# One-hot tiles built for four quads at a time, key sums by halving, and routing keys turned one group earlier

## The reference, cut to what matters

```python
q = (xb @ w_q).reshape(128, 8, 2, 128)
s = einsum('bhpd,hpkd->bhpk', q, sub_keys)      # two score lists of 128 keys per head
sv, si = top_k(s, 16)
cand = sv[:, :, 0, :, None] + sv[:, :, 1, None, :]
cv, ci = top_k(cand, 16)
i1 = take_along_axis(si[:, :, 0], ci // 16)
i2 = take_along_axis(si[:, :, 1], ci % 16)
idx = i1 * 128 + i2                             # 8 heads x 16 experts per token
gate = softmax(cv)
act = gelu(einsum('bhkd,bd->bhk', u_emb[idx], xb))
out = einsum('bhk,bhkd->bd', gate * act, v_emb[idx])
```

## Time and profile before

| what | us |
|---|---|
| median of 3 runs | 2011.41 |
| lowest and highest of them | 2003.05, 2014.95 |
| the profiled execution | 2016.21 |
| its span, first to last instruction | 2014.5 |
| PE, DVE, ACT, POOL busy | 1926.0, 1462.6, 751.0, 738.8 |
| mean granted TensorE clock | 0.981 of full speed |

### The profile page before, as it was taken

One profiled execution on the slowest core, in us unless ns is written; L12 is line 12 of the kernel. 1 busy time (PEld: TensorE's weight loads), 2 busy tenths in 40 slices (PEclk: granted clock), 3 DMA queues, 4 the chain that ended last, 5 costly groups with the idle time before them and its releaser, 6 DMA issues.

```text
span 2014.5 us, 35532 instructions
## 1 busy us (share of the span) xinstructions
PE 1926.0 (96%) x14267; PEld 1758.4 (87%) x14267; DVE 1462.6 (73%) x2696; ACT 751.0 (37%) x953; POOL 738.8 (37%) x600
## 2 busy tenths in 40 slices
PE   9998987888999999999999999998899999999997
PEld 8998976767459999988888888888899999999997
DVE  6616664775247778878887997885698788888887
ACT  6334543443032133445444545543223332233323
POOL 8235737560023101322322241221488544333440
PEclk9999988999999999999999999999999999999999
DMA  6212210020231135677888797779999999999993
GB/s 204 64 45 76 66 40 2 9 92 12 71 142 59 68 132 193 237 275 276 330 326 295 274 366 268 287 282 341 356 367 362 386 364 362 360 365 368 358 336 124
DMA packets 179180, 450.11 MB, mean 223 GB/s; under 512 B 15729, under 2 KB 92273, under 8 KB 168817
## 3 DMA queue, kind: packets, MB, share of 16 engines
q1 hardware_dynamic: 125472, 240.77, 34.5%
q0 software_dynamic: 42496, 151.03, 20.3%
q10 hardware_dynamic: 11088, 56.63, 6.9%
HBM read 383.26 MB, written 65.07 MB: 223 GB/s over the span
## 4 chain that ended last, share of the span: by engine, by line
PE 77%; DVE 9%; POOL 4%; DMA 3%; ACT 3%; issue 3%; SPq 1%; ACTq 0%; DVEq 0%; POOLq 0%
PE bank L2028 27%; PE bank L1943 23%; PE bank L1897 5%; PE bank L1360 5%; PE bank L1849 3%; DMA v_raw<-in_pv 2%; PE bank L1952 2%; PE bank L1380 1%; DMA sca<-in_pu_rows,pick 1%; PE bank L1919 1%; DVE u_lo L2602 1%; DVE sca L2608 1%; DVE pre L2166 1%; SPq L595 1%; PE bank L1570 1%
## 5 line engine op out<-in xcount | busy, mean ns | idle before, releaser
L1943 PE MATMUL bank<-xhi,u_hi 128*128 128x448 f32 x1008 | 380.0, 377 | 5.2 <-ACT actb L1236 5.2
L1943 PE MATMUL bank<-xhi,u_lo 128*128 128x448 f32 x1008 | 369.8, 367 | 0.0
L1943 PE MATMUL bank<-xlo,u_hi 128*128 128x448 f32 x1008 | 368.7, 366 | 0.0
L842 POOL DMA_INDIRECT sca<-in_pu_rows,pick x128 | 173.1, 1352 | 527.9 <-DVE sdot L2608 414.1
L2028 PE MATMUL bank<-w_hi,v_hi 128*128 128x416 f32 x1024 | 358.3, 350 | 6.1 <-DVE w_lo L2861 5.4
L2028 PE MATMUL bank<-w_lo,v_hi 128*128 128x416 f32 x1024 | 357.8, 349 | 0.0
L2028 PE MATMUL bank<-w_hi,v_lo 128*128 128x416 f32 x1024 | 357.7, 349 | 0.0
L1289 ACT ACTIVATE v_hi<-v_raw 128x4096 fp32r<-128x4096 f32 x32 | 115.9, 3621 | 394.1 <-PE bank L2028 355.7
L2867 DVE TENSOR_TENSOR v_lo<-v_raw,v_hi 128x4096 fp32r<-128x4096 f32 x32 | 141.6, 4425 | 95.7 <-ACT v_hi L1289 95.7
L2602 DVE TENSOR_TENSOR u_lo<-u_raw,u_hi 128x2048 fp32r<-128x2048 f32 x64 | 146.5, 2290 | 86.8 <-ACT u_hi L1208 82.5
L1943 PEld LDWEIGHTS bank<-xhi,u_hi 128*128 128x128 f32 x1008 | 189.7, 188 | 19.6 <-issue 5.6
(11 more groups left out here) (698 smaller groups left out, 3728.7 us busy)
## 6 DMA issues: line engine op xcount, KB each, us to landing
u_raw<-in_pu SPq DMA_DIRECT2D x64, 1024.0 KB, 5.1
v_raw<-in_pv SPq DMA_DIRECT2D x128, 512.0 KB, 8.6
act_scratch<-actb ACTq DMA_DIRECT2D x64, 448.0 KB, 6.1
wts<-act_scratch SPq DMA_DIRECT2D x32, 896.0 KB, 6.9
gate_scratch<-gst ACTq DMA_DIRECT2D x13, 2048.0 KB, 9.0
gring<-gate_scratch SPq DMA_DIRECT2D x32, 832.0 KB, 13.4
wring<-in_w_q SPq DMA_DIRECT2D x4, 2048.0 KB, 8.9
wp_raw<-in_w_in SPq DMA_DIRECT2D x7, 1024.0 KB, 5.4
```

The lines of the kernel that those rows point to most:

```text
L842: pool.indirect_dma_start(rows_u[s % RING], None, pu_rows[:, :], bass.IndirectOffsetOnAxis(pick[:, s:s + 1], 0)).then_inc(s_row[s % RING], 16)
L1943: ins = mm(bank[b][:, 0:DS], lhsT, rhs[:, 0:DS], **on)
```

## The change

1. One block of one-hots is made for four quads: `hot_b` and `hot_e` have 2048 elements in one operation, `hot_a` is made for two quads at a time, and "hots_ready" goes up by two. The rings grow with it: `hot_b` holds 8 quads (from 4), `hot_a` 4 (from 2), `hot_e` 4 (from 2).
2. `hot_b` and `hot_a` move to SBUF addresses that held query data used up by then; `hot_e` takes their old place.
3. `sum_keys` is one reduce no more, but four additions of 2048, 1024, 512 and 256 elements, each waiting for the one before.
4. PE turns the keys of position 1 ahead of group 11, and those of position p+1 ahead of the last group of position p. PE's code for positions 1 and 2 is written out, where it was a loop over 8 groups.

```diff
-        hot_b = sb("hot_b", [128, 8, 128, 2], f16, scope=first)
-        hot_a = sb("hot_a", [128, 2, 2, 2, 128, 2], f16, scope=first)
-        hot_e = sb("hot_e", [128, 4, 128, 2], f16, scope=first)
+        hot_e = sb("hot_e", [128, 8, 128, 2], f16, scope=first)
+        sb("gap_hot", [128, 1536], scope=first)
...
+        hots = ExitStack()
+        hot_b = sb("hot_b", [128, 16, 128, 2], f16, scope=hots)
+        hot_a = sb("hot_a", [128, 4, 2, 2, 128, 2], f16, scope=hots)
...
+            def turn_keys(pos):
+                t = ORDER[pos]
+                n = FTILES[t][1]
+                pe.wait_ge(S("routed"), ROUTED[pos])
+                for a, src in enumerate((isel[0:n, 0, :], isel[0:n, 1, :], gate[0:n, t, :])):
+                    ins = pe.transpose(bank[4][:, 128 * a:128 * a + n], src, ident[0:n, 0:n])
+                ins.then_inc(S("hk_done"), 1)
...
+            for e in range(GU):
+                dots(0, 2, HEAD0 - 2, e)
+            turn_keys(1)
+            for e in range(GU):
+                dots(0, 2, HEAD0 - 1, e)
+            for pos in range(1, 5):
+                for g in range(G0[pos], G0[pos] + GROUPS_OF[pos]):
+                    if pos < 4 and g + 1 == G0[pos + 1]:
+                        turn_keys(pos + 1)
+                    first_q, last_q = QUAD0[g - HEAD0], QUAD0[g - HEAD0 + 1]
+                    half = (last_q - first_q) // 2
+                    for e in range(GU):
+                        dots(0, 2, g, e)
+                        for quad in range(first_q + half * e, first_q + half * e + half):
+                            gate_quad(quad)
...
-                    if k % 2 == 0:
...
-                        if quad >= 4:
-                            dve.wait_ge(S("gmat_done"), quad - 2)
-                        TT(hot_b[:, s:s + 4, :, :], every, both[1], ALU.is_equal)
+                    if k % 4 == 0:
...
+                        if quad >= 8:
+                            dve.wait_ge(S("gmat_done"), quad - 4)
+                        TT(hot_b[:, s:s + 8, :, :], every, both[1], ALU.is_equal)
...
-                    if quad >= 2:
-                        dve.wait_ge(S("gmat_done"), quad - 1)
...
+                    if k % 2 == 0:
+                        if quad >= 4:
+                            dve.wait_ge(S("gmat_done"), quad - 2)
+                        rows_e = hot_e[:, 2 * (k % 4):2 * (k % 4) + 4, :, :]
+                        two = hot_a[:, quad % 4:quad % 4 + 2, :, :, :, :].rearrange("p q r a n j -> p (q r) a n j")
+                        TT(two, rows_e.unsqueeze(2).to_broadcast([128, 4, 2, 128, 2]),
+                           hk_g[:, 2 * k:2 * k + 4, :, :].unsqueeze(3).to_broadcast([128, 4, 2, 128, 2]), ALU.mult
+                           ).then_inc(S("hots_ready"), 2)
...
-                link(dve.tensor_reduce(isel[0:n, :, :].rearrange("p a (k r) -> p (a k) r", r=2),
-                                       hot[0:n, :].rearrange("p (k j r) -> p k r j", k=128, j=16), AX.X, ALU.add))
+                places = hot[0:n, :].rearrange("p (k j r) -> p k j r", k=128, j=16)
+                for half in (8, 4, 2):
+                    link(TT(places[:, :, 0:half, :], places[:, :, 0:half, :], places[:, :, half:2 * half, :], ALU.add))
+                link(TT(isel[0:n, :, :].rearrange("p a (k r) -> p (a k) r", r=2), places[:, :, 0, :], places[:, :, 1, :], ALU.add))
```

More of the change, by code:

```diff
@@ L39 @@
 TAIL = 3
+ROUTED = [1, 2, 3, 4, 5]
 G0 = [HEAD0 + sum(GROUPS_OF[:t]) for t in range(5)]
@@ L344, in hybrid_step @@
         query.close()
+        hots = ExitStack()
+        hot_b = sb("hot_b", [128, 16, 128, 2], f16, scope=hots)
+        hot_a = sb("hot_a", [128, 4, 2, 2, 128, 2], f16, scope=hots)
+        hots.close()
         first.close()
@@ L1944, in dots, with gate_quad @@
                 ins.then_inc(S("dots_done"), 1)
-            def gate_quad(i, t, k):
-                pe.wait_ge(S("hots_ready"), i * 16 + (32 * t + k + 1))
-                pe.wait_ge(S("gmat_copied"), i * 16 + (32 * t + k + 1))
+            def gate_quad(k):
+                pe.wait_ge(S("hots_ready"), k + 1)
+                pe.wait_ge(S("gmat_copied"), k + 1)
                 for j in range(4):
                     for part in range(2):
-                        ins = mm(bank[5 + k % 2][:, 128 * j:128 * j + 128], hot_b[:, 2 * (k % 4) + j // 2, :, j % 2],
-                                 hot_a[:, k % 2, j // 2, part, :, j % 2], start=part == 0, stop=part == 1)
+                        ins = mm(bank[5 + k % 2][:, 128 * j:128 * j + 128], hot_b[:, 2 * (k % 8) + j // 2, :, j % 2],
+                                 hot_a[:, k % 4, j // 2, part, :, j % 2], start=part == 0, stop=part == 1)
                 ins.then_inc(S("gmat_done"), 1)
@@ L1972, in _ @@
                 dots(0, 2, 1, e)
-            with pe.Fori(0, HEAD0 // 2 - 1) as i:
+            def turn_keys(pos):
[5 more added lines that the diff above has]
+                ins.then_inc(S("hk_done"), 1)
+            with pe.Fori(0, HEAD0 // 2 - 2) as i:
                 for q in range(2):
@@ L1976, in _ @@
                         dots(i, 2, 2 + q, e)
[L1977 to L2000, removed]
+            for e in range(GU):
[13 more added lines that the diff above has]
+                            gate_quad(quad)
             for g in range(GATED_END, UG):
                 for e in range(GU):
-                    dots(0, 8, g, e)
+                    dots(0, 2, g, e)
             pe.sem_inc(S("sum_done"), 2 * KD)
@@ L2664, in one_hots @@
                     quad = t0 // 4 + k
-                    s = 2 * (quad % 4)
-                    if k % 2 == 0:
-                        both = [hk_ab[:, a, 4 * k:4 * k + 8].rearrange("p (r j) -> p r j", j=2).unsqueeze(2)
-                                .to_broadcast([128, 4, 128, 2]) for a in range(2)]
-                        every = lanes[:, :, :].unsqueeze(1).to_broadcast([128, 4, 128, 2])
-                        if quad >= 4:
-                            dve.wait_ge(S("gmat_done"), quad - 2)
-                        TT(hot_b[:, s:s + 4, :, :], every, both[1], ALU.is_equal)
+                    s = 2 * (quad % 8)
+                    if k % 4 == 0:
+                        both = [hk_ab[:, a, 4 * k:4 * k + 16].rearrange("p (r j) -> p r j", j=2).unsqueeze(2)
+                                .to_broadcast([128, 8, 128, 2]) for a in range(2)]
+                        every = lanes[:, :, :].unsqueeze(1).to_broadcast([128, 8, 128, 2])
+                        if quad >= 8:
+                            dve.wait_ge(S("gmat_done"), quad - 4)
+                        TT(hot_b[:, s:s + 8, :, :], every, both[1], ALU.is_equal)
                         if quad:
```

## The result

The changed kernel takes **2030.76 us** in the median of 4 runs (2029.24 to 2036.34), the kernel before 2012.7 (2003.05 to 2014.95). The ratio is 1.009, with a 95% interval of 1.0062 to 1.0117: slower, and by more than the 0.5% that the prediction took as what can be told from no change. The forecast was 2015.8, with 2026 as the upper end. The same comparison made once more later, beside other runs of the kernel before, gave 1.0053 (1.0032 to 1.0074): slower too, but there the 0.5% lies inside the interval.

A forecast was written before the change was run, and what follows sets the result against it. PE was taken to bound the kernel. The terms, 2 x (0.97 + 1.59) + 0.97 - 1.64 = +4.4 us, gave 2020.6 for the profiled execution and a median of 2015.8; range 2004 to 2025.4, 2026 with the unrolling's bad end.

The forecast's parts named there:

- What bounds the kernel: PE, busy 1926.0 of 2014.5 us; DVE's saved 11 us count nothing, covered by 59.5 us of waits for `u_hi`.
- Price of a doubled operation: On DVE, 2048 elements take 1.22 us, 1.14 to a successor, 1.26 to a waiting one; 11 us of DVE time saved.
- the additions: On DVE in j = 11: four additions hold it 2.9 us where the reduce held it 4.44.
- Price of the longer block: On DVE, 3.67 us until the first quad can start, for 2.08: 1.59 us later.
- j = 10: Group in positions 1, 2 and 3: the long block makes the first quad's stall 1.80 us, from 0.21.
- j = 11 and the head of position 4: No stall at j = 11 in positions 1 to 3; position 4's first quad just in time, -1.64 us.
- j = 14: Group in positions 1 and 2: the stall of 1.57 us becomes 3.16, +1.59 each.
- In positions 2 and 3 the first block gets longer too, behind four dots; I find some 0.5 us left, and count 0: First quads of positions 2 and 3: some 0.5 us of room for the longer block, so 0 us.
- rival C: Gathers collide with long blocks (first quads of positions 2, 3; j = 14): 9.6 us more, 2025.4; chance 0.13.
- Addresses: 0; the new places are idle: Moving the one-hot buffers to other SBUF addresses costs 0 us.
- Written-out code, 0: PE's written-out code in positions 1 and 2 costs 0; bad end 0.1 us per group, +3.

The follow-up runs named there:

- e10: Kernel before with 1.46 us of useless DVE work ahead of the block of every even group: 2027.88 us for 2016.19, ratio 1.0067.
- e3: Kernel before with the four additions in place of the reduce, nothing else: ratio 1.0002.
- e4: Kernel before with PE's code written out and the keys turned one group ahead: ratio 1.0002.
- e7: Kernel before with the new SBUF addresses and the longer rings, but blocks of two quads: ratio 1.0001.
- e2: Kernel before with the doubled one-hot operations, their rings and places alone: 2027.21 us for 2016.02, ratio 1.0070.
- e11: The changed kernel once more, beside other runs of the kernel before: 2026.82 us for 2016.19, ratio 1.0053.
- e13: Kernel before with the three one-hot buffers at the new addresses, old rings, a single execution: dots of 5.00 and 5.04 us in the gated stage.
- e1: Kernel before with PE's code for positions 1 and 2 written out, nothing else: 2018.12 us for 2016.02, ratio 1.0028.
- e5: The changed kernel with the short blocks, rings and places of before, against the kernel before: 2013.75 us for 2015.13, ratio 0.9988.

## Why the prediction was wrong

- **What bounds the kernel**: right. PE does, and DVE's saved time went into its waits for `u_hi`.
- **Price of a doubled operation**: right, 1.22 long, 1.15 and 1.30 to the next for 1.14 and 1.26. Of the additions only the last was off, 0.43 for some 0.35. DVE's busy time fell by 18 us, and none of it reached the end. The Trainium skill's rule that few large tiles pay the fixed latency less often (VectorE: DVE Perf Modes, section on the TRN2 errata) holds for that busy time, and says nothing of the time of the kernel.
- **Price of the longer block**: right. First quad 3.74 us after the block's start (947.95 to 951.69), forecast 3.67. j = 10 cost +4.8 us, as forecast; e10, with stalls of 1.64 to 1.66 there, shows that lateness alone does it.
- **j = 11 and the head of position 4**: right, each alone in e3 and e4.
- **j = 14**: right in kind, +2.5 for +3.2. The two parts are uneven, +0.8 and +1.7, and e7 shows 0.88 and 1.90 there without any change to DVE's order of work, so how near the sum came is partly luck.
- **"In positions 2 and 3 the first block gets longer too, behind four dots; I find some 0.5 us left, and count 0"**: this step failed. At the head of position 2 the fourth dot waited 4.19 us for its row and the quad was 3.75 late. In e2 it was 4.15, in e11 4.76. The head of position 3, counted 0 too, was on time. So rival C, which had 0.13, was right at one of its four places and not in its price of 9.6. The step failed on the row and not on the block: in e10 a block nearly as late as this one (1.46 us for 1.59) cost nothing there. A margin of 0.5 us was set against row waits of up to 2.4 us, and why a row should not come later than that was not asked; by the rows above, 0.2 us in the order of POOL and DVE made the difference between before and after.
- **No term for the clock**: behind stalls of 3.75 and 3.42 us PE ran at its lower level, 3.1 us more. I had noted a granted clock of 1.00 in this stage and not asked what a longer stall would do to it. The Trainium skill (TensorE: Matmul & The Clock Gate, Part 1) says that idleness brings it down; the prediction did not weigh it.
- **"Addresses: 0; the new places are idle"**: wrong by 2.6 us; e7 and e13 show it without the long operations.
- **Written-out code, 0**: not settled. e1 gave 1.0028, but e4 and e5, with the same form of code, 1.0002 and 0.9988; both also hold the early turn, which wins 1.6 us.

With the three missed terms, 3.8 + 3.1 + 2.6, the forecast of +4.4 would have been +13.9, where the two profiled executions differ by 13.0. The difference of the medians is 18.1 in the first comparison (four runs of each, spread over 7 and 12 us) and 10.6 in e11 (10 runs from 2014.15 to 2034.79, 24 of before from 2007.91 to 2021.43); in the two traces of the changed kernel the gated stage accounts for 13.2 and 13.4. The median of e11 moved by less than its gated stage and that of the first comparison by more, and the value stage, with the same code, varies by 7 us from trace to trace; what makes it vary stays open.

## What to carry to other kernels

Here, fusing small operations of an engine that isn't the bound saved busy time and made the first consumer wait for the whole. So: look up what stands ahead of each long operation, and put it where nothing is late. Slack should be compared with the largest wait seen in the trace, not with its mean, and even that is no bound: the largest wait of a dot for its row in the gated stage was 2.4 us in the trace before and 4.2 after. A stall over 3 us mostly cost its length and then the clock, here 8 times of 10. And 0.3% came from the cheap parts of the change and from spreading the work ahead of the late quads evenly, without the part that gave it its name.

## What the runs showed of the hardware that was not expected

**The clock after short stalls.** In the gated stages of all these runs PE's stalls up to 2.0 us were never followed by half clock, and none lies between 2.0 and 2.26. Of eight between 2.26 and 2.95 us three were (2.26, 2.46 and 2.95), and of ten from 3.05 to 4.76 us eight; the two that were not are 3.05 in e11 and 3.09 in e10. The price was 1.3 to 2.8 us each time. Which of two stalls of the same length is followed by a fall was not found.

**Matmuls and addresses.** Moving `hot_b`, `hot_a` and `hot_e` to other SBUF addresses lengthened matmuls that don't read them from 4.99 to 5.00 and 5.04 us per 24, in turn for e = 0 and e = 1, in five kernels out of five. With the longer rings 4.96 for 4.91 remained behind the gated stage too, where nobody writes one-hots. What in the chip does this was not found.

**Gather instructions beside DVE.** The late row of position 2 is one case of something that all fourteen traces show. Between 830 and 1400 us POOL issues 117 or 118 gathers for the dots in each. All 213 of these instructions that began while DVE was idle, or in the last 0.08 us of its operation, took 0.93 or 0.94 us. Of the 757 that began while DVE ran a dot, 749 took 0.94 us and what was left of the dot, within 0.15 us, so up to 1.99. In six they began less than 0.05 us behind the dot, took 0.94, and the dot was 1.27 to 1.30 long instead of 1.22; two took 3.97. The three that began 0.06 to 0.09 behind `split_u`, which is 2.29 long, took 3.0; one that began 0.04 behind it took 0.94. So in these traces the order of two starts decides who waits for whom, and the price is the rest of DVE's operation.
